# Twenty of the 22 weight tiles of each up-projection as seven block products of 256 columns

## The reference

```python
def conv_ffn(h, w_up, conv_w, conv_b, w_down):
    gate, val = jnp.split(h @ w_up, 2, axis=-1)          # h 512x1024, w_up 1024x5632
    gate = causal_depthwise_conv(gate, conv_w) + conv_b   # three taps along the tokens
    return (jax.nn.silu(gate) * val) @ w_down             # w_down 2816x1024

for layer in range(2):
    x = x + mixer(rms_norm(x, mix_norm_g[layer]))
    x = x + conv_ffn(rms_norm(x, ffn_norm_g[layer]), ...)
return rms_norm(x, final_norm_g)
```

## Time and profile before

| what | value |
|---|---|
| median of three runs | 1221.3 us (1220.79 to 1221.42) |
| span of the profiled execution | 1219.5 us |
| median of the runs less that span | 1.8 us (no time of its own is listed for the profiled execution beside its span) |
| TensorE busy | 99% of the span |
| VectorE, ScalarE, GpSimd busy | 42%, 41%, 47% |
| up-projection of layer 0 after its first tile | 286.5 to 515.0 us |
| up-projection of layer 1 after its first tile | 864.2 to 1092.7 us |

### The profile page before, as it was taken

One profiled execution on the slowest core, in us unless ns is written; L12 is line 12 of the kernel. 1 busy time (PEld: TensorE's weight loads), 2 busy tenths in 40 slices (PEclk: granted clock), 3 DMA queues, 4 the chain that ended last, 5 costly groups with the idle time before them and its releaser, 6 DMA issues.

```text
span 1219.5 us, 16989 instructions
## 1 busy us (share of the span) xinstructions
PE 1207.9 (99%) x6230; PEld 1036.3 (85%) x6230; DVE 507.8 (42%) x900; ACT 501.6 (41%) x743; POOL 567.4 (47%) x509
## 2 busy tenths in 40 slices
PE   8999999999999999999999999999999999999997
PEld 7999999888888888888888889888888888888886
DVE  7878777653211212323241375635321212232325
ACT  6665555544322223423342366344332322343234
POOL 2435544335444444566645332613544444456662
PEclk9999999999999999999999999999999999999999
DMA  7222222113222222222223211301322222222221
GB/s 270 92 98 95 79 70 70 67 38 121 103 103 103 73 99 103 104 84 89 104 87 121 87 70 57 117 36 39 123 98 103 103 92 86 97 103 104 75 98 70
DMA packets 17325, 113.71 MB, mean 93 GB/s; under 512 B 1920, under 2 KB 2304, under 8 KB 4608
## 3 DMA queue, kind: packets, MB, share of 16 engines
q1 hardware_dynamic: 16416, 110.20, 25.2%
q10 hardware_dynamic: 864, 2.88, 0.7%
HBM read 110.98 MB, written 2.10 MB: 93 GB/s over the span
## 4 chain that ended last, share of the span: by engine, by line
PE 95%; DVE 2%; ACT 1%; issue 1%; DMA 0%; DVEq 0%; SPq 0%; ACTq 0%
PE ps L1600 38%; PE ps L1893 16%; PE ps L1681 9%; PE ps L1543 7%; PE ps L1572 3%; PE ps L2024 2%; PE ps L1722 2%; PE ps L1645 2%; PE ps L2004 2%; PE ps L1590 2%; PE ps L1650 1%; PE ps L1928 1%; PE ps L1708 1%; PE ps L1491 1%; PE ps L1734 1%
## 5 line engine op out<-in xcount | busy, mean ns | idle before, releaser
L316 POOL TENSOR_TENSOR w_lo<-w_raw,w_hi 128x512 fp32r<-128x512 f32 (+1 forms) x329 | 462.5, 1437 | 515.5 <-ACT w_hi L413 459.5
L413 ACT ACTIVATE w_hi<-w_raw 128x2048 fp32r<-128x2048 f32 (+1 forms) x93 | 171.9, 1848 | 309.1 <-PE ps L1600 155.2
L1600 PE MATMUL ps<-hT_hi,w_hi 128*128 128x512 f32 x688 | 267.7, 389 | 0.0
L1600 PE MATMUL ps<-hT_hi,w_lo 128*128 128x512 f32 x688 | 267.7, 389 | 0.0
L1600 PE MATMUL ps<-hT_lo,w_hi 128*128 128x512 f32 x688 | 267.6, 389 | 0.0
L1600 PEld LDWEIGHTS ps<-hT_hi,w_hi 128*128 128x128 f32 x688 | 129.1, 188 | 26.8
L1600 PEld LDWEIGHTS ps<-hT_lo,w_hi 128*128 128x128 f32 x688 | 129.1, 188 | 26.8
L1600 PEld LDWEIGHTS ps<-hT_hi,w_lo 128*128 128x128 f32 x688 | 129.1, 188 | 26.7
L1235 DVE TENSOR_TENSOR hT_lo<-region,hT_hi 128x2048 fp32r<-128x2048 f32 (+1 forms) x22 | 58.9, 2684 | 144.0 <-ACT hT_hi L686 144.0
L1205 DVE SCALAR_TENSOR_TENSOR qk<-ps,vec,qk 128x511 f32<-128x511 f32 x44 | 33.0, 750 | 200.1 <-ACT qk L660 200.1
L660 ACT ACTIVATE qk<-ps,vec 128x512 f32<-128x512 f32 x44 | 34.3, 780 | 175.5 <-PE ps L1600 166.3
(11 more groups left out here) (278 smaller groups left out, 2102.3 us busy)
## 6 DMA issues: line engine op xcount, KB each, us to landing
w_raw<-weights SPq DMA_DIRECT2D x99, 1024.0 KB, 4.8
gain<-gains ACTq DMA_DIRECT2D x4, 512.0 KB, 3.5
x<-x_in SPq DMA_DIRECT2D x3, 512.0 KB, 7.5
out<-region SPq DMA_DIRECT2D x3, 512.0 KB, 2.7
w_raw<-weights SPq DMA_DIRECT2D x2, 384.0 KB, 5.6
w_raw<-weights SPq DMA_DIRECT2D x1, 768.0 KB, 8.6
cst<-consts SPq DMA_DIRECT2D x1, 640.0 KB, 10.2
x<-x_in ACTq DMA_DIRECT2D x1, 512.0 KB, 4.1
```

The costliest lines, as they stand in the source:

```text
L316: ins = pool.tensor_tensor(w_lo[:, slot, cols], w_raw[:, slot, cols], w_hi[:, slot, cols].bitcast(f32), ALU.subtract)
L413: sc.activation(w_hi[:, slot, 0:used], w_raw[:, slot, 0:used], ACT.Copy).then_inc(w_hi_ready, 1)
L1600: ins = pe.matmul(bank, w[:, slot, k * pitch + 128 * s:k * pitch + 128 * s + 128], h[:, k:k + 1, :], start=k == 0 and n == 0, stop=k == KT ...
```

## The change

The up-projection is turned into a product of 2x2 blocks. For 256 output channels, the weight tile A (256 channels by 1024 inputs) is cut into halves of 128 channels and halves of 512 inputs; the input B (1024 by 512 tokens) into halves of 512 inputs and halves of 256 tokens. In place of eight block products there are seven (Winograd's form of Strassen's scheme): S1 = A21 + A22, S2 = S1 - A11, S3 = A11 - A21, S4 = A12 - S2; T1 = B12 - B11, T2 = B22 - T1, T3 = B22 - B12, T4 = B21 - T2 (the sign of T4 as in the code). Each block product is 4 x 3 = 12 matmuls with 256 moving columns. This is done for the tiles 2 to 21 of each layer; tiles 0 and 1 are multiplied as before, from the new order of columns in the tile (`in_tile`), and into other banks. Around it:

- ScalarE copies the turned input from PSUM to SBUF (`copy_raw`, 8 copies a layer), rounds the T blocks once a layer, copies `w_hi` with 1536 columns a tile, rounds S1 (512 columns) and S2 to S4 (1536), and copies the first product to SBUF (`copy_p1`). The gate's first tap is read from SBUF.
- VectorE makes the T blocks once a layer; per tile four sums of 512 columns (`block_sums`), the low half of S4 (`fourth_low`), and four additions that combine the products (`combine_block`). The taps and the product with the value now read `z` in SBUF (`convolve`, `multiply`).
- GpSimd makes six low halves of 512 columns a tile in place of four (`block_lows`).
- The loads of `gain` move from before the feed-forward part into its last pair, and the halves of the first down tile go to `hT_hi` and `hT_lo` in place of `first_hi` and `first_lo`.

The core of the diff, by engine (GpSimd, ScalarE, VectorE, TensorE, then the order of the weights). Lines that only go away are those of `mlp` printed above; the rounding of the T blocks, once a layer, and the semaphores are left out:

```diff
+z = region[:, 13312:15104]
+p1 = (region[:, 15104:15360], vec[:, 0:256])
...
+with pool.Fori(1, PAIRS) as i:
+    for half in range(2):
+        tile = 2 * i + (half - 2)
+        pool.wait_ge(w_hi_ready, 2 * i + (n0 + half + 1))
+        for a in (0, 512):
+            low(w_lo[:, half, a:a + 512], w_raw[:, half, a:a + 512], w_hi[:, half, a:a + 512])
+        pool.wait_ge(s_summed[l], tile + 1)
+        low(w_lo[:, half, 1024:1536], w_raw[:, half, 1024:1536], w_hi[:, half, 1024:1536])\
+          .then_inc(w_lo_ready, 1)
+        pool.wait_ge(s_high[l], 2 * tile + 1)
+        low(w_lo[:, half, 1536:UNIT], s1_raw[half][:, :], w_hi[:, half, 1536:UNIT]).then_inc(s_low[l], 1)
+        pool.wait_ge(s_high[l], 2 * tile + 2)
+        for a in (0, 512):
+            low(s_lo[half][:, a:a + 512], s_raw[half][:, a:a + 512], s_hi[half][:, a:a + 512])\
+              .then_inc(s_low[l], 1)
...
+def copy_raw(l, t, before):
+    for g in range(2):
+        sc.wait_ge(turn_lo, 8 * before + 2 * t + g + 1)
+        sc.activation(raw_h[:, 4 * g:4 * g + 4, t * 128:(t + 1) * 128],
+                      ps[:, MLP_TURN[t] + g, :].rearrange("p (j n) -> p j n", j=4), ACT.Copy)\
+          .then_inc(raw_copied[l], 1)
...
+def block_high(i, half):
+    sc.wait_ge(mm_done, 8 * i + 4 * (n0 + half - 1))
+    sc.wait_ge(w_loaded[half], 16 * i + 16 * (n0 // 2 + 1))
+    sc.activation(w_hi[:, half, 0:1536], w_raw[:, half, 0:1536], ACT.Copy).then_inc(w_hi_ready, 1)
+def sum_highs(i, half):
+    sc.wait_ge(s_summed[l], 2 * i + (half - 1))
+    sc.activation(w_hi[:, half, 1536:UNIT], s1_raw[half][:, :], ACT.Copy).then_inc(s_high[l], 1)
+    sc.activation(s_hi[half][:, :], s_raw[half][:, :], ACT.Copy).then_inc(s_high[l], 1)
+def copy_p1(i, half):
+    sc.wait_ge(product_done[l], 4 * i + (2 * half - 3))
+    sc.activation(p1[half], ps[:, 4 * half + 3, 0:256], ACT.Copy).then_inc(p1_copied[l], 1)
...
+def pair(i, last=False):
+    block_high(i, 1)
+    copy_p1(i, 0)
+    sum_highs(i, 1)
+    if last:
+        split_after(n1 - 2)
+    else:
+        block_high(i + 1, 0)
+    copy_p1(i, 1)
+    if not last:
+        sum_highs(i + 1, 0)
+    sc.wait_ge(combined[l], 2 * i + 1)
+    for s in range(2):
+        gate_start(i, s, (z1, z2)[s])
+    silu(i)
...
+if last:
+    first_highs()
+    sc.preload_act_table_set("sqrt_and_others")
+    split_after(n1 - 1)
+    load_gain()
...
+def block_sums(i, half):
+    a11, a12, a22, a21 = (w_raw[:, half, 512 * j:512 * j + 512] for j in range(4))
+    s1, (s2, s3, s4) = s1_raw[half][:, :], (s_raw[half][:, 512 * j:512 * j + 512] for j in range(3))
+    ve.wait_ge(mm_done, 8 * i + 4 * (n0 + half - 1))
+    ve.wait_ge(w_loaded[half], 16 * i + 16 * (n0 // 2 + 1))
+    first = own.mark(ve.tensor_tensor(s1, a21, a22, ALU.add))
+    ve.tensor_tensor(s3, a11, a21, ALU.subtract)
+    own.wait(first)
+    own.link(ve.tensor_tensor(s2, s1, a11, ALU.subtract))
+    ve.tensor_tensor(s4, a12, s2, ALU.subtract).then_inc(s_summed[l], 1)
+def fourth_low(i, half):
+    ve.wait_ge(s_high[l], 4 * i + (2 * half - 2))
+    ve.tensor_tensor(s_lo[half][:, 1024:1536], s_raw[half][:, 1024:1536],
+                     s_hi[half][:, 1024:1536].bitcast(f32), ALU.subtract).then_inc(s4_low[l], 1)
+def two(bank):
+    return ps[:, bank, :].rearrange("p (a n) -> p a n", a=2)
+def combine_block(i, half, last=False):
+    b = 4 * half
+    if not last:
+        ve.wait_ge(product_done[l], 4 * i + (2 * half - 2))
+    else:
+        ve.wait_ge(mm_done, 4 * n1)
+    ve.wait_ge(p1_copied[l], 2 * i + (half - 1))
+    own.link(ve.tensor_tensor(z[:, 512:1536].rearrange("p (a n) -> p a n", a=2)[:, :, 0:256], two(b),
+                              p1[half].unsqueeze(1).broadcast_to([128, 2, 256]), ALU.add))
+    ve.wait_ge(mm_done, 8 * i + 4 * (n0 + half + 1))
+    u34 = z[:, 1280:1792].rearrange("p (a n) -> p a n", a=2)
+    own.link(ve.tensor_tensor(u34, two(b + 1),
+                              z[:, 1024:1280].unsqueeze(1).broadcast_to([128, 2, 256]), ALU.add))
+    ve.tensor_tensor(z[:, 0:1536].rearrange("p (a n) -> p a n", a=2)[:, :, 0:256], two(b + 2), u34, ALU.add)
+    ve.tensor_tensor(z[:, 256:512], ps[:, b + 1, 256:512], z[:, 1280:1536], ALU.add)\
+      .then_inc(combined[l], 1)
+def multiply(i):
+    ve.wait_ge(combined[l], 2 * i + 2)
     for s in range(2):
         ve.wait_ge(silu_ready[l], 2 * i + s + 1)
+        ve.tensor_tensor(act[:, ds(2 * i + s, 1), :], (z1, z2)[s].unsqueeze(1), qk[:, s:s + 1, :],
+                         ALU.mult).then_inc(act_done[l], 1)
...
+def pair(i, last=False):
+    block_sums(i, 1)
+    fourth_low(i, 1)
+    if not last:
+        block_sums(i + 1, 0)
+    combine_block(i, 0)
+    if not last:
+        fourth_low(i + 1, 0)
+    convolve(i, (z1, z2))
+    if last:
+        first_lows()
+    combine_block(i, 1, last)
+    multiply(i)
...
+def in_tile(blocked, k, s):
+    if not blocked:
+        return 256 * k + 128 * s
+    return 128 * k if s == 0 else 1024 + 128 * ((k + 4) % KT)
...
+PARTS = {1: ("A11", "B11", 3, 0), 2: ("A12", "B21", 0, 0), 3: ("S4", "B22", 2, 256),
+         4: ("A22", "T4", 2, 0), 5: ("S1", "T1", 1, 256), 6: ("S2", "T2", 0, 256), 7: ("S3", "T3", 1, 0)}
+def product(half, p):
+    left, right, bank, col = PARTS[p]
+    (wh, wl), (th, tl) = weights_of(half, left), moving(right)
+    for k in range(4):
+        for n, (w, t) in enumerate(((wh, th), (wh, tl), (wl, th))):
+            ins = pe.matmul(ps[:, 4 * half + bank, col:col + 256], w[:, 128 * k:128 * k + 128], t[:, k, :],
+                            start=k == 0 and n == 0, stop=k == 3 and n == 2)
+    return ins
+def block_tile(i, half, first=False, last=False):
+    pe.wait_ge(combined[l], 2 * i + (half - 1))
+    pe.wait_ge(w_lo_ready, 2 * i + (n0 + half + 1))
+    product(half, 1).then_inc(product_done[l], 1)
+    product(half, 2)
+    for p in (7, 3, 5, 6, 4) if last else (3, 5, 6, 4, 7):
+        if p == 3:
+            pe.wait_ge(s4_low[l], 2 * i + (half - 1))
+        elif p in (5, 6, 7):
+            pe.wait_ge(s_low[l], 6 * i + 3 * (half - 2) + (p - 4))
+        if first and p != 3:
+            pe.wait_ge(t_low[l], {5: 1, 6: 2, 4: 3, 7: 4}[p])
+        ins = product(half, p)
+        if p == (7 if last else 6):
+            ins.then_inc(product_done[l], 1)
+    ins.then_inc(mm_done, 4)
...
+block_tile(1, 0, first=True)
+block_tile(1, 1)
+with pe.Fori(2, LAST) as i:
+    block_tile(i, 0)
+    block_tile(i, 1)
+block_tile(LAST, 0)
+block_tile(LAST, 1, last=True)
...
+pe.wait_ge(combined[l], 2 * LAST + 1)
+down_tile(0, [(0, four, True, False, every)], False, n1 + 1, 4)
+pe.wait_ge(combined[l], 2 * LAST + 2)
...
+def blocks(w):
+    w = w.reshape(KT, 128, -1)
+    return [tiles(np.concatenate([w[a:a + 4, :, c + f:c + f + 128] for f, a in ((0, 0), (0, 4), (128, 4), (128, 0))]))
+            for c in range(0, w.shape[2], 256)]
```

More of the change, by code:

```diff
@@ L498, in norm @@
                 root(k, 2, eps[:, 0:1])
+                before_mlp = k in (1, 3)
+                if before_mlp:
+                    copy_raw(k // 2, 0, turns[0])
                 square(k, 3)
@@ L654, in mlp, with gate_start @@
                 n1 = n0 + FT
[L656 to L663, removed]
+                def gate_start(i, s, source):
+                    col = V_CONV + l * FT * 4 + 4 * s
+                    sc.activation(qk[:, s, :], source, ACT.Identity, scale=vec[:, ds(8 * i + (col + 2), 1)],
+                                  bias=vec[:, ds(8 * i + (col + 3), 1)]).then_inc(conv_started[l], 1)
@@ L680, in mlp @@
+                sc.wait_ge(mm_done, 4 * (n0 + 2))
+                sc.activation(hT_hi[:, 0:4, 256:512], t3_raw, ACT.Copy).then_inc(t_high[l], 1)
+                with sc.Fori(1, LAST) as i:
                     pair(i)
-                pair(FT // 2 - 1, first_highs)
+                pair(LAST, last=True)
                 def halves(u0, kt, slot, count=4):
@@ L950, in split_part, with lows @@
                     ins.then_inc(w_lo_ready, 1)
-            def lows(b):
+            def lows(b, banks):
                 t, g = b // 2, b % 2
@@ new lines, in mlp @@
+                ve.wait_ge(raw_copied[l], 8)
+                b11, b12, b21, b22 = (raw_h[:, 4 * k:4 * k + 4, 256 * t:256 * t + 256] for k in range(2) for t in range(2))
+                first = own.mark(ve.tensor_tensor(t_raw[0][:, :, :], b12, b11, ALU.subtract))
+                own.wait(first)
+                ve.sem_inc(t_summed[l], 1)
+                ve.tensor_tensor(t3_raw, b22, b12, ALU.subtract).then_inc(t_summed[l], 1)
+                own.link(ve.tensor_tensor(t_raw[1][:, :, :], b22, t_raw[0][:, :, :], ALU.subtract))
@@ new lines, in mlp @@
+                ve.sem_inc(t_summed[l], 1)
+                ve.tensor_tensor(t_raw[2][:, :, :], b21, t_raw[1][:, :, :], ALU.subtract).then_inc(t_summed[l], 1)
+                for j in range(3):
+                    ve.wait_ge(t_high[l], j + 1)
+                    ve.tensor_tensor(t_lo[j][:, :, :], t_raw[j][:, :, :], t_hi[j][:, :, :].bitcast(f32), ALU.subtract)\
```

(19 more changed lines are left out.)

180 lines of the change are left out of this document (112 added, 68 removed).

## The result

| kernel | median, us | lowest to highest | span, us | mean granted clock |
|---|---|---|---|---|
| before | 1221.34 | 1220.79 to 1221.42 | 1219.5 | 1.00 |
| after | 1318.86 | 1317.91 to 1319.02 | 1316.1 | 0.959 |

The ratio is 1.0798, with a 95% interval of 1.0782 to 1.0813: 8% slower. The forecast was 1320.5 us.

A forecast was written before the change was run, and what follows sets the result against it. VectorE's round, stretched by exclusion with GpSimd, was taken to bound the loop: 26.6 against 21.76 us a pair, ten pairs plus 1.2 giving 49.6 a layer, 99 for two, hence 1320.5 us; range 1245 to 1350.

The forecast's parts named there:

- TensorE, matmuls of 256 columns: Up-projection: 84 matmuls at 0.120 us replace 48, 10.08 us a tile, saving 0.80 us a tile.
- odd fourth low: wait, block: VectorE's low half of S4, odd tile: waits some 2.1 us for ScalarE's two copies, then 0.5 for GpSimd.
- even tile's four sums, blocks: VectorE's sums of the next even tile meet GpSimd in full stride, blocked 1.0 to 1.1 us each, 4.2 together.
- first two taps, blocks: In `convolve`, GpSimd blocks VectorE's first two taps 1.0 us each; the last two are free.
- two products, blocks: In `multiply`, GpSimd blocks VectorE's two products by 0.9 and 1.1 us.
- a pair: Two up-projection tiles take VectorE's round: 15.7 work, 8.8 blocks, 2.1 waiting for ScalarE, 26.6 us against 21.76 before.
- around the loop, a layer: Outside the pairs: copies, T blocks and the first down tile cost 1.2 us a layer, T blocks delaying tile 2.
- the 1.2 us before each even tile: TensorE stands still 6.4 us a pair: about 5.3 before each odd tile and 1.2 before each even one.
- The bound of 15 us a layer: Upper limit for work around the loop, were all of it on the path uncovered: 8 x 0.59 + 10 us.
- A: Loop: the shared SBUF port alone sets the pace, 22.3 us a pair, 1234.5 us; chance 0.12 including values up to forecast.
- B: Loop: GpSimd and VectorE rarely exclude each other, TensorE sets 20.2 us a pair, kernel 1192 us; chance 0.09.
- C: Loop: TensorE's clock drops in the new waits, odd tiles at 1.2 GHz, 31.5 us a pair, 1417 us; chance 0.07.

The follow-up runs named there:

- e1: Changed kernel with GpSimd's lows cut from 512 to 32 columns in the blocked tiles, TensorE multiplying the high half instead: 1199.65 us.
- e2: Changed kernel with one of the two inputs of each block sum and of the fourth low read from PSUM instead of SBUF: 1256.97 us.
- e3: Changed kernel with GpSimd's lows in the blocked tiles made in pieces of 256 columns, twice the instructions for the same work: 1282.40 us.
- e6: Changed kernel with only the ten value tiles of a layer as block products, the gate tiles plain: 1209.54 us, ratio 0.9901 to the kernel before.
- e7: Changed kernel with ScalarE's first rounded copies for the down-projection made before the SiLUs in the last pair: 1310.91 us.
- e4: Changed kernel with 30 small matmuls before each odd blocked tile's wait, so that TensorE isn't idle: 1318.73 us.
- e5: Changed kernel with ScalarE making the next pair's odd-tile rounded copy before the gates and SiLUs, not after them: 1334.0 us.

## Why the prediction came out right, step by step

One mechanism carried the result, and e1, e2 and e3 show it from three sides: take GpSimd's time away and the loop is TensorE's, take one SBUF input away and that instruction is free, halve GpSimd's pieces and the turn shortens by half a piece. That the forecast of the whole is only 1.6 us off the median is luck: two of its terms missed, by 6.8 and 5.7 us a layer, in opposite directions.

| step, us | predicted | measured |
|---|---|---|
| TensorE, matmuls of 256 columns | 0.120 us, 10.08 a tile | 0.1201 (e1's piece), 9.99 (e6's) |
| odd tile's sums | free, 0.60 apart | 0.68 long, 463.51 to 466.1 |
| odd fourth low: wait, block | 2.1, 0.5 | 2.07, 0.40 |
| even tile's four sums, blocks | 4.2 | 1.67 to 1.78 each, 4.3 |
| first two taps, blocks | 2.0 | 1.3 |
| two products, blocks | 2.0 | 1.75 |
| waits for the gate and between taps | 0 | 0.6 |
| a pair | 26.6 | 26.27 |
| ten pairs against before, a layer | +48.4 | +41.6 |
| around the loop, a layer | +1.2 | +6.9 |
| a layer | +49.6 | +48.5 |

**The bound and the order of the wait.** TensorE's waits have GpSimd's w_lo as releaser, 11 in a layer, behind VectorE's L1335: as said. They are 3.4 us on the average (37.9 in 11) and 4.8 at the longest, not 5.3, and the 1.2 us before each even tile is not there at all (in the round shown the even tile runs straight on from the odd one at 479.07). The missing part comes back as slow matmuls: the odd tile takes 11.55 us (467.52 to 479.07), not 10.08. VectorE is busy 87% of the round (22.98 of 26.30 us), close to the 90% that I had named.

**The loop: too high by 6.8 us.** The steady pair is 0.33 shorter than stepped (3.3 us in ten): the taps are blocked less, since the first meets the end of a GpSimd instruction (1.27 us, not 1.75), and the products by 0.25 less; together this outweighs 0.6 us of waits for ScalarE's gates and between taps that I had left out. The remaining 3.5 us lie at the start. I multiplied the steady round by ten, but the first pair is shorter: from the start of its even tile to ScalarE's row of the chain (298.72 to 309.11) it takes 10.4 us, in the steady loop 13.9 (the tile after the odd one shown starts at 479.07, the next row at 466.69 + 26.27). Behind the first block tile VectorE has no blocks of a pair before it to combine, and no taps; its two products still read PSUM there (1.27 us for two at 300.30). The loop as measured runs from 298.72 to the end of the last block tile at 557.97, 259.2 us against 217.6.

**Around the loop: too low by 5.7 us.** "The first down tile waits for `act_lo`, which is in VectorE's round" was priced at nothing. It is a wait of 3.7 us (557.97 to 561.64; 2.7 in layer 1), and behind it the down stage runs 99.80 instead of 97.92 us. Of these 1.9 us, 1.6 are the lowered clock (e6 and e7 have 98.2 at a clock of 1.00). With the 1.4 us by which the first block tile comes late (298.72, against 286.48 + 10.88), that is 6.9. The bound of 15 us a layer in the prediction did cover it; the value picked, 1.2, was the mis-sized term.

Two things stand in the chain before the down stage. The last pair's taps have two SBUF inputs and run beside GpSimd's lows for the down-projection. VectorE, then GpSimd, in the changed kernel:

```profile
552.36 1.67 DVE L1322 SCALAR_TENSOR_TENSOR qk<-region,vec,qk 128x510 f32<-128x510 f32 x1
553.95 1.78 DVE L1319 SCALAR_TENSOR_TENSOR qk<-region,vec,qk 128x511 f32<-128x511 f32 x1
555.76 1.66 DVE L1322 SCALAR_TENSOR_TENSOR qk<-region,vec,qk 128x510 f32<-128x510 f32 x1
```

```profile
550.48 6.39 POOL L350 TENSOR_TENSOR w_lo<-w_raw,w_hi 128x512 fp32r<-128x512 f32 x4
```

The four taps take 6.1 us, where they would take 3.0 unblocked. And after the last of them VectorE waits 1.7 us for ScalarE's rounded copies, which stand behind the last SiLU. e1 left GpSimd's lows of the down-projection whole, so its last taps are blocked alike (0.91, 1.67, 1.78 and 1.67 us from 492.27), and its wait says nothing against the exclusion. e7 took away the second thing only: the down stage starts 1.8 us earlier a layer and takes 98.20 us, 3.4 us a layer or 6.8 in the profiled spans (7.9 by the medians). The wait itself fell by more, to 0.6 and 1.2 us, but in layer 0 this is in part because the last odd tile happened to run slow for longer (546.54 to 552.0, against 546.46 to 549.4) and ended 1.3 us later. What unblocked taps would give there was not tried.

The 1.4 us before the first block tile can be read from the trace. VectorE makes the lows of the T blocks and the four taps of pair 0 before its first sums (294.52 to 297.23), GpSimd's low of A22 follows them (297.31, 1.27 us), and TensorE starts at 298.72. In e1, where that low is thin, TensorE starts at 297.60, 0.2 us late.

**The rivals.** A (the port alone, 22.3 a pair): it would need GpSimd never to wait, and GpSimd waits 3.16, 0.63 and 4.22 us in the pair shown. The reason that I gave against A, the waits on results of its own, is not what hands the port over: the first two even sums don't wait for each other, and they too start 1.68 us apart (469.20 and 470.88). B: e1 is nearly B's kernel, with a loop free of the exclusion, and took 1199.65, so B's 1192 was itself some 3.9 us a layer too low; the 3.1 us wait at the loop's end and the slower start of the down stage are what it left out. C: the mechanism of the clock exists, and its price in the loop is nothing. In the pair shown the slow stretch is 15 matmuls, not an odd tile, and costs 1.5 us, taken from a wait that follows anyway; e4 removed it without a change in time. Its price was outside the loop, where nothing follows that waits: 1.6 us at the down stage.

**Where the blind spot lay.** e2's and e5's misses have the same root. In a loop of two engines that take turns, an edit that frees one of them moves the other's work in time. e2 freed 5 us and kept 3 of them, because GpSimd no longer stood still beside all of the last taps. e5 removed 1.8 us of blocks and paid 2.3 of waiting. Each was clear after stepping the round again, and neither from the list of blocks alone.

## What to carry to other kernels

Before a saving of TensorE's work is paid for with elementwise work, step one round of the helpers through, each instruction with its place beside the other engine's: here 15.7 and 15.1 us of work that fit into 20.2 side by side made a round of 26.3. Halve such a scheme before dropping it: with only one tile of each pair as blocks, the same idea gains 1%. And price a loop's two ends by themselves, above all the last thing that the next stage waits for: here it cost 5.3 us a layer that the sum had at nothing.

## What the runs showed of the hardware

- VectorE with two SBUF inputs against GpSimd's SBUF-to-SBUF subtract waits for whole instructions, for tensor_tensor and scalar_tensor_tensor alike: sums of 0.68 against 1.77 us, taps of 0.75 against 1.75 (e2). With 256-column GpSimd instructions the same sum takes 1.22 (e3). (The Trainium skill, "SBUF — State Buffer", section "Who interferes with whom", describes an exclusive lock held for an instruction's length. The durations agree.)
- After a wait of 3.4 us TensorE's clock was at 1.2 GHz for 3.4 us of work (0.57 in the 4 us from 467) and at 2.4 GHz again after it. The length varies: after waits of 3.7 and 4.0 us before the last odd tile the slow work lasted 2.9 us (changed kernel) and 5.5 us (e7). A wait of 1.5 us after small matmuls left the clock at 1.00 (e4), and one of 0.6 as well (e7).
- One GpSimd subtract of 256 columns took 0.71 us at the least (e3), one of 512 took 1.26: halving the pieces costs GpSimd some 13%, and the kernel still fell from 1318.9 to 1282.4 us.
- I had not expected that slow matmuls in a waiting loop would cost nothing (e4) while 3.7 us of waiting at a stage's start would bring another 1.6 us with it (e7).
